# A decoder layer on one core: hidden tiles 4 and 5 computed as a pair, and another order of work in the opening

## The reference, cut to what matters

```
h = rms_norm(x, g_mix)
q, k, v, u, gate_a, gate_s = split(h @ w_in)       # 1024 -> 4096
attn_out = stick_breaking_attention(rms_norm(q), rms_norm(k), v) @ w_attn_out
y = gelu(s5(u));  ssm_out = (y @ w_glu_val) * sigmoid(y @ w_glu_gate)
x = x + (sigmoid(gate_a) * attn_out + sigmoid(gate_s) * ssm_out) @ w_out
x = x + square(relu(rms_norm(x, g_mlp) @ w_up)) @ w_down      # 1024 -> 4096 -> 1024
x = x + (p @ w_ple) * sigmoid(rms_norm(x, g_ple) @ w_ple_gate)
```

## Time and profile before

| what | value |
|---|---|
| median of 3 runs | 929.46 us (929.38 to 929.7) |
| the profiled execution | 929.17 us, span 927.5 us |
| PE busy | 912.6 us, 98% of the span, 7414 matmuls |
| DVE busy | 603.9 us, 65% |
| ACT busy | 442.1 us, 48% |
| POOL busy | 87.3 us, 9% |
| chain that ended last | PE 92%, DVE 3%, ACT 2%, issue 1% |

### The profile page before, as it was taken

The page is one execution under the profiler, slowest core; times in us unless marked ns, Lnnn a source line. Parts: engine busy times, 40 slices in busy tenths (PEclk is TensorE's granted clock), DMA queues, the critical chain, the costliest instruction groups (busy, mean ns, idle before and its releaser), DMA issues.

```text
span 927.5 us, 17663 instructions
## 1 busy us (share of the span) xinstructions
PE 912.6 (98%) x7414; PEld 886.1 (96%) x7414; DVE 603.9 (65%) x815; ACT 442.1 (48%) x663; POOL 87.3 (9%) x142
## 2 busy tenths in 40 slices
PE   6999999999999999999999999999999999999998
PEld 5999999999999889999999999999999999999998
DVE  6589699511777746475568666666676666778453
ACT  7546323223876544444356544444444444446532
POOL 5190032201001210100000000000000000000000
PEclk9999999999999999999999999999999999999999
DMA  9531554824523576522323222322323223242203
GB/s 234 126 87 44 149 166 105 192 74 154 131 71 96 197 277 213 170 70 69 92 69 92 90 84 83 89 90 91 91 75 92 87 90 92 91 137 71 69 5 99
DMA packets 134694, 102.19 MB, mean 110 GB/s; under 512 B 18560, under 2 KB 124408, under 8 KB 134584
## 3 DMA queue, kind: packets, MB, share of 16 engines
q1 hardware_dynamic: 129096, 83.38, 30.7%
q0 software_dynamic: 5424, 17.65, 6.0%
q10 hardware_dynamic: 96, 0.04, 0.0%
HBM read 88.71 MB, written 12.21 MB: 109 GB/s over the span
## 4 chain that ended last, share of the span: by engine, by line
PE 92%; DVE 3%; ACT 2%; issue 1%; DMA 0%; ACTq 0%; DVEq 0%
PE dense L2278 65%; PE banks L2278 20%; PE scoreA L2278 3%; PE banks L2434 2%; PE dense L2434 1%; PE scoreB L2278 1%; DVE Llo L1735 1%; ACT t L1616 1%; DVE t L2102 1%; ACT whi L1323 1%; DVE Ssum L1711 0%; DMA xtok<-in_x_sample 0%; DVE wlo L1735 0%; DVE sm L2160 0%; ACT yh L1662 0%
## 5 line engine op out<-in xcount | busy, mean ns | idle before, releaser
L1735 DVE TENSOR_TENSOR wlo<-wraw,whi 128x1024 fp32r<-128x1024 f32 (+1 forms) x139 | 152.6, 1102 | 104.2 <-ACT whi L1323 91.9
L2278 PE MATMUL dense<-hid,whi 128*128 128x256 f32 (+1 forms) x1024 | 176.6, 294 | 0.1
L2278 PE MATMUL dense<-act_hi,whi 128*128 128x256 f32 (+1 forms) x736 | 168.1, 298 | 1.4 <-issue 1.4
L2278 PE MATMUL dense<-act_hi,wlo 128*128 128x256 f32 (+1 forms) x736 | 164.6, 294 | 0.3 <-DVE wlo L1735 0.3
L2278 PE MATMUL dense<-act_lo,whi 128*128 128x256 f32 (+1 forms) x736 | 164.4, 294 | 0.0
L2278 PEld LDWEIGHTS dense<-hid,whi 128*128 128x128 f32 x1024 | 152.5, 188 | 0.5 <-issue 0.4
L1323 ACT CAST whi<-wraw 128x1024 fp32r<-128x1024 f32 x100 | 110.1, 1103 | 45.6 <-PE banks L2278 44.1
L2278 PEld LDWEIGHTS dense<-act_hi,whi 128*128 128x128 f32 x736 | 123.9, 188 | 4.8 <-issue 4.1
L2278 PEld LDWEIGHTS dense<-act_hi,wlo 128*128 128x128 f32 x736 | 124.6, 188 | 0.5 <-DVE wlo L1735 0.5
L2278 PEld LDWEIGHTS dense<-act_lo,whi 128*128 128x128 f32 x736 | 124.7, 188 | 0.0
L2278 PE MATMUL dense<-hid,wlo 128*128 128x256 f32 (+1 forms) x512 | 108.8, 294 | 0.0
(11 more groups left out here) (366 smaller groups left out, 1571.2 us busy)
## 6 DMA issues: line engine op xcount, KB each, us to landing
wraw<-in_w_in SPq DMA_DIRECT2D x32, 512.0 KB, 4.9
wraw<-in_w_up SPq DMA_DIRECT2D x32, 512.0 KB, 4.0
wraw<-in_w_down SPq DMA_DIRECT2D x32, 512.0 KB, 3.6
gates_spill<-gst POOLq DMA_DIRECT2D x16, 288.0 KB, 3.1
page<-in_cache_k SPq DMA_DIRECT2D x16, 256.0 KB, 7.9
page<-in_cache_v SPq DMA_DIRECT2D x16, 256.0 KB, 7.5
wraw<-in_w_out SPq DMA_DIRECT2D x8, 512.0 KB, 3.8
wraw<-in_w_ple_gate SPq DMA_DIRECT2D x8, 512.0 KB, 3.6
```

Source lines behind the costliest of these rows:

```text
L1735: return nc.vector.tensor_tensor(out=lo, in0=whole, in1=f32(hi), op=ALU.subtract)
L2278: return nc.tensor.matmul(out, lhsT, rhs, start=start, stop=stop, skip_group_check=True)
```

## The change: what it does

Two parts are changed together.

**Pair.** FIRSTPAIR becomes 4, so hidden tiles 4 and 5 are also one pair and there are 14 pairs. The units behind up 3 are now: D0, D1, pair 4, D2, pair 6, D3, pair 8, D4, D5, and so on: pairs 4 and 6 have one down unit behind each, the later ones two as before. In the event list, up 3 is followed by a flush (which holds the first two weight blocks of pair 4), by three of the four blocks of both halves of D0, and then by xpair 3, xsplit 2, rscale 2, xsplit 3, rscale 3, and only then by the rest of D0 half 0 and of half 1, rscale 6 and 7, and D1.

**Opening.** EVICT has an order for each half: 0, 2, 1, 3, 4, 6, 5, 7 for half 0, as before for half 1. ACT's copy of the first weights stands behind two tiles, not three. GpSimd subtracts 768 of the 1024 columns of the first `wlo`, DVE the other 256. GpSimd's tables come behind that. PE's first unit is reordered, and the second has an order of its own (all high x high, then high x low, then low x high).

```diff
-EVICT = (0, 2, 4, 6, 1, 3, 5, 7)
+EVICT = ((0, 2, 1, 3, 4, 6, 5, 7), (0, 2, 4, 6, 1, 3, 5, 7))
@@ units_of
     for f in range(8):
-        for i in range(0, 4, 2):
-            m, d = 4 * (f + 1) + i, [("down", 8 * f + 2 * n, 4, 2) for n in (i, i + 1)]
-            if m < FIRSTPAIR:
-                us += [("up", m, 8, 1), d[0], ("up", m + 1, 8, 1), d[1]]
-            else:
-                us += ([("pair", m, 8, 1), ("pair2", m + 1, 8, 1)] if f < 7 else []) + d
+        downs = [("down", 8 * f + 2 * n, 4, 2) for n in range(4)]
+        wide = [[("pair", m, 8, 1), ("pair2", m + 1, 8, 1)] if m < 32 else [] for m in (4 * f + 4, 4 * f + 6)]
+        if f == 0:
+            us += downs[0:2] + wide[0] + downs[2:3] + wide[1] + downs[3:4]
+        else:
+            us += wide[0] + downs[0:2] + wide[1] + downs[2:4]
-FIRSTPAIR = 6
+FIRSTPAIR = 4
@@ schedule_of
-    def pair():
+    def pair(downs):
...
-        for j in range(2):
+        for j in range(2 * downs):
             half_unit()
-            event("hidlow", m + j)
-        for j in range(2):
-            half_unit()
+            if j < 2:
+                event("hidlow", m + j)
...
         if half == 1:
+            event("pool_lo", 0)
             event("split_lo", 0)
-        for turn, k in enumerate(EVICT):
-            if half == 0 and turn == 3:
+        for turn, k in enumerate(EVICT[half]):
+            if half == 0 and turn == 2:
                 event("split_hi", 0)
...
     event("xsplit", 1)
     unit()
+    flush()
+    for j in range(2):
+        event("hpart", n[0], j, 0, 3)
     event("xpair", 3)
     event("xsplit", 2)
     event("rscale", 2)
-    unit()
     event("xsplit", 3)
     event("rscale", 3)
     half_unit(split_first=False)
-    flush()
-    half_unit()
+    half_unit(split_first=False)
     event("rscale", 6)
     event("rscale", 7)
-    unit(2)
+    unit()
     for m in range(FIRSTPAIR, 32, 2):
         if m == LASTHID - 8:
             event("inv")
-        pair()
+        pair(2 if m >= 8 else 1)
@@ gpsimd
+                if k == "pool_lo":
+                    pool.wait_ge(w_hi, turn["split", 0])
+                    tt(wlo[:, wslot(0), 0:LOW0], wraw[:, 0, 0:LOW0], f32(whi[:, wslot(0), 0:LOW0]),
+                       ALU.subtract).then_inc(count.up(pool_steps), 1)
+                    reached["w0_lo"] = count.last
+                    tables()
@@ vector
+                elif k == "split_lo":
+                    vector.wait_ge(w_hi, turn["split", 0])
+                    vector.wait_ge(*reached["w0_lo"])
+                    lower(wlo[:, wslot(0), LOW0:], wraw[:, 0, LOW0:],
+                          whi[:, wslot(0), LOW0:]).then_inc(count.up(w_lo), 1)
@@ tensor, first_unit
+                tensor.wait_ge(w_hi, turn["split", 0])
+                tensor.wait_ge(h_lo, EVICT[0].index(1) + 2)
+                high(0, 0, KT)
+                low_x(0, False)
+                high(1, 0, KT // 2)
+                tensor.wait_ge(w_lo, turn["split", 0])
+                low_w(0, 0, KT, True)
+                low_w(1, 0, KT // 2, False)
+                high(1, KT // 2, KT)
+                low_w(1, KT // 2, KT, False)
+                ins = low_x(1, True)
+            def second_unit():
+                tensor.wait_ge(w_hi, turn["split", 1])
+                slot = jobs["m", 1, 0][0] - DENSE
+                wh, wl = [wview(w, wslot(1), 1) for w in (whi, wlo)]
+                for turn_, (w, x) in enumerate(((wh, act[0]), (wh, act[1]), (wl, act[0]))):
+                    if turn_ == 2:
+                        tensor.wait_ge(w_lo, turn["split", 1])
+                    for k in range(KT):
+                        for c0, c1 in CUT:
+                            ins = mm(product_of(slot, c0, c1), w[:, k, 0:P], x[:, k, c0:c1],
+                                     start=turn_ == 0 and k == 0, stop=turn_ == 2 and k == KT - 1)
```

More of the change, by code:

```diff
@@ L1078, in _ @@
             sync.wait_ge(y_stored, 16 * 13)
+        LOW0 = 6 * P
         N_PARAMS = 14 + 2 * 4
@@ L1133, in _ @@
                                  ident[0:32, 0:32].unsqueeze(1).to_broadcast([32, 4, 32])).then_inc(count.up(pool_steps), 1)
[L1134 to L1157, removed]
             def load_x2(t):
@@ L1167, in load_p, with tables @@
                 pool.dma_start(ptok[0:n, t % 2, :], src).then_inc(x2_in[t % 2], 16)
+            def tables():
+                nc.gpsimd.memset(nrm[:], 1.0).then_inc(count.up(pool_steps), 1)
+                for half in range(2):
+                    nc.gpsimd.memset(f32(nrmr[half][:]), 0.0).then_inc(count.up(pool_steps), 1)
+                nc.gpsimd.memset(f32(selr[:]), 0.0).then_inc(count.up(pool_steps), 1)
+                sflat = sel[:, :, :].rearrange("r p c -> r (p c)")
+                nc.gpsimd.memset(sflat, 1.0).then_inc(count.up(pool_steps), 1)
+                pool.wait_ge(*count.last)
+                nc.gpsimd.affine_select(out=sflat, in_=sflat, compare_op=ALU.is_ge, fill=0.0, base=0,
+                                       pattern=[[1, 8 * P]], channel_multiplier=-64).then_inc(count.up(pool_steps), 1)
+                pool.wait_ge(*count.last)
+                nc.gpsimd.affine_select(out=sflat, in_=sflat, compare_op=ALU.is_ge, fill=0.0, base=63,
+                                       pattern=[[-1, 8 * P]], channel_multiplier=64).then_inc(count.up(pool_steps), 1)
+                pool.wait_ge(*count.last)
+                for r in (0, 32):
+                    nc.gpsimd.tensor_copy(selr[r:r + 16, :, :], sel[:, :, :]).then_inc(count.up(pool_steps), 1)
+                pool.wait_ge(*count.last)
+                nc.gpsimd.tensor_copy(stat[:, 2, 0:1], ident[:, 0:1]).then_inc(count.up(consts_ready), 1)
+                for row in range(SB):
+                    src = i["sb_bias"][0:1, 2 * (row // 2):2 * (row // 2) + 2].rearrange("a (h o) -> (a h) o", o=1)
+                    pool.dma_start(sbias[16 * row:16 * row + 16, :],
+                                   src.unsqueeze(1).to_broadcast([2, ST, 1])).then_inc(sbias_in, 16)
+                pool.dma_start(pti[:, :], i["page_table"].rearrange("b (n o) -> o (b n)", o=1)).then_inc(table_in, 16)
@@ L1169, in _ @@
             for e in schedule:
                 k, a = e[0], e[1:]
-                if k == "s5sq":
+                if k == "pool_lo":
[4 more added lines that the diff above has]
+                    tables()
+                elif k == "s5sq":
                     pool.wait_ge(s5_bb, 1)
@@ L1474, in _ @@
                     if m % 2:
-                        scalar.wait_ge(h_lo, KT * half + EVICT.index(m - 1) + 2)
+                        scalar.wait_ge(h_lo, KT * half + EVICT[half].index(m - 1) + 2)
                     nc.scalar.activation(act[0][:, m, c0:c0 + 2 * P], xview(half, m), ACT.Copy,
@@ L1883, in _ @@
                     c0 = 2 * P * half
-                    vector.wait_ge(h_hi, KT * half + EVICT.index(m) + 1)
+                    vector.wait_ge(h_hi, KT * half + EVICT[half].index(m) + 1)
                     nc.vector.scalar_tensor_tensor(out=act[1][:, m, c0:c0 + 2 * P], in0=xview(half, m),
@@ L1891, in _ @@
                             count.upto(*read(("xturned", half))), 1)
-                elif k in ("split", "split_lo"):
+                elif k == "split_lo":
[3 more added lines that the diff above has]
+                          whi[:, wslot(0), LOW0:]).then_inc(count.up(w_lo), 1)
+                elif k == "split":
                     split(a[0])
@@ L2303, in first_unit @@
                 wh, wl = [wview(w, 0, 0) for w in (whi, wlo)]
[L2305 to L2322, removed]
@@ L2323, in first_unit, with high, low_x @@
-                ins.then_inc(full_of(("m", 0, 0)), 1)
+                def high(half, n0, n1):
+                    c0, c1 = CUT[half]
+                    for n in range(n0, n1):
+                        k = EVICT[half][n]
+                        tensor.wait_ge(h_hi, KT * half + n + 1)
+                        mm(product_of(slot, c0, c1), wh[:, k, 0:P], act[0][:, k, c0:c1], start=n == 0)
+                def low_x(half, stop):
+                    c0, c1 = CUT[half]
+                    for n, k in enumerate(EVICT[half]):
+                        tensor.wait_ge(h_lo, KT * half + n + 2)
+                        ins = mm(product_of(slot, c0, c1), wh[:, k, 0:P], act[1][:, k, c0:c1],
+                                 stop=stop and n == KT - 1)
+                    return ins
@@ new lines, in low_w @@
+                def low_w(half, n0, n1, stop):
+                    c0, c1 = CUT[half]
+                    for n in range(n0, n1):
+                        k = EVICT[half][n]
+                        mm(product_of(slot, c0, c1), wl[:, k, 0:P], act[0][:, k, c0:c1], stop=stop and n == KT - 1)
+                tensor.wait_ge(w_hi, turn["split", 0])
[3 more added lines that the diff above has]
+                high(1, 0, KT // 2)
@@ new lines, in first_unit @@
+                tensor.wait_ge(w_lo, turn["split", 0])
[4 more added lines that the diff above has]
```

(8 more changed lines are left out.)

## The result

| kernel | median us | range, runs | profiled execution | mean granted clock |
|---|---|---|---|---|
| before | 929.42 | 929.02 to 929.7, 4 | 929.17 (span 927.5) | 1.00 |
| changed | 935.88 | 935.22 to 936.3, 4 | 935.22 (span 933.5) | 0.996 |

The ratio is 1.007 (95% interval 1.0058 to 1.0083): slower by 6.5 us. The prediction was 934.7.

The account below looks back on a forecast made before the run. PE, busy 98% of the span, was taken as the bound, so any new wait costs in full. -1.54 + 6.0 + 1.4 - 0.7 = +5.2 us gave a median of 934.7 us, range 931.0 to 937.0.

Parts of the forecast that it names:

- Matmuls removed, -1.54: Tiles 4 and 5 as one pair on PE: 11.10 us in place of 12.64, so -1.54 us.
- The wait, +6.0: Between D0 and D1 half 0, PE waits for DVE's late addition of D0 half 0 into R: 6.0 us.
- Behind the wait, nothing: From D1 and pair 4 on: no second wait, blocks lowered in time, weight loads cost nothing.
- PE's speed, +1.4: PE's matmuls behind the wait run slowly after the idle time: +1.4 us, bounds 0 and 2.5.
- The opening, -0.7: PE's first unit ends at 22.3 us, second unit earlier than 23.00: -0.7 us, bounds 0 and -1.4.
- GpSimd's share, no cost: Opening: GpSimd's 768-column subtraction takes 0.8 to 3.5 us, taken as under 3.0, so DVE is not held up.
- The late tables: GpSimd's tables start some 2.5 us later and end near 25; first PE user after 36 us, so no cost.
- The median: Whole kernel: 934.4 us for the profiled execution, plus 0.29 to the median of the runs, 934.7.
- the one at full pace: Rival: the wait before D1 comes, but PE restarts at once at full pace: 933.2 us; chance 0.28.
- the late GpSimd one: Rival: GpSimd's subtraction takes 5 us, DVE goes on 2 us later, opening +1.2: 936.6 us; chance 0.08.
- the one with a part of the wait hidden: Rival: DVE gets through work ahead earlier, hiding part of the wait: 929.5 to 932.5 us; chance 0.07.
- the rival of a short wait: Rival: wait before D1 short or absent, so faster, deciding at 2.2 us; 927.2 without any wait; chance 0.12.

Follow-up runs that it names:

- repaired kernel: Changed kernel with D0's two DVE additions ahead of xpair 3, PE's D0 reordered, rscale 6 and 7 behind pair 4, its blocks 4 to 6 behind its first product: 926.95 us.
- filler run: Changed kernel plus 40 extra matmuls of 288 rows into an unused PSUM bank between D0 and D1, result unread: 933.35 us.
- opening's order alone: Kernel before with the opening's new orders but without GpSimd's share, DVE subtracting all 1024 columns of the first low weights: 929.11 us.
- opening alone: Kernel before with the whole opening part, GpSimd's share included, and the pairs of before: 928.53 us.
- pair part alone: Kernel before with only the pair's edits and the opening of before: 936.12 us.
- kernel with 2.3 us: Changed kernel with both DVE additions of D0 ahead of xpair 3 and PE's D0 blocks reordered so half 0 ends earlier: 931.39 us.

## Why the prediction was right, step by step

The mechanism that makes the loss, the wait and the fallen clock behind it, is shown. That the size taken for the clock came near is in part luck.

- **Matmuls removed, -1.54.** The sum closes to 0.2 us with it. In the two profiles: -0.46 (lead at up 3's end, 492.57 against the earlier trace rows), +5.96 wait, +1.86 slow matmuls, -1.54 make +5.8; the difference of the profiled executions is 6.05. The repaired kernel, without wait, is 2.2 us under before, the -1.54 and -0.7 of the prediction.
- **The wait, +6.0.** 5.96 measured, in the place named, behind the addition named. DVE's list was also right line by line: shifted by the lead of 0.46, the forecast has xpair 3 done at 499.8, xsplit 3 and rscale 3 at 503.9, and the measured rows stand at 499.80 and 503.91. So no part of the wait was hidden. The experiments moved it to 3.9, 1.8 and 0 by moving what stands ahead of the addition.
- **Behind the wait, nothing.** Right for the changed kernel: no second wait shows. It was right only because of the wait itself: with the wait gone, 2.3 us turned up in pair 4, at ACT's psave copy. The prediction had said that pair 4's blocks have time; it did not name that copy.
- **PE's speed, +1.4.** The mechanism was right, the size too small: 1.86 at matmul starts, of which the filler run leaves 1.78 to the clock, and 2.2 to 2.5 between the medians. That 1.4 came so near is in part luck, since the 1.2 us it leaned on is not the price of slow transposes. The transposes were slow, as the durations of equal ones in the kernel before show (ns: least, median, most):

```profile
L2434 PE MATMUL dense<-ident,xtok x16: 417/418/473, 8.7 to 11.9; 128*128 128x128 f32 x16
L2434 PE MATMUL banks<-ident,xtok x16: 272/273/447, 12.2 to 14.2; 128*128 128x128 f32 x16
```

But both stretches that were compared are held by DVE's row tiles too. The first, 3.49 us, ends when the third row tile is scaled, at 12.12. In the run with the opening's order alone the first 16 were quicker, and PE then waited for that tile:

```profile
8.76 3.25 PE L2475 MATMUL dense<-ident,xtok 128*128 128x128 f32 x16 [0.47 <-DVE xtok L1871]
12.25 2.31 PE L2475 MATMUL banks<-ident,xtok 128*128 128x128 f32 x16 [0.24 <-DVE xtok L1871]
```

The second 16 start 7.57 us after the first square in both (12.18 - 4.61 and 12.25 - 4.68), so there the slow clock cost as good as nothing. The second stretch, 2.31 us, holds a pause for the fourth row tile (starts at 13.12 and then 13.40, where 0.11 is the step).
- **A slip in the same paragraph.** "PE is idle for 0.24 of 7.10 us busy" has the earlier trace rows the wrong way round: PE is busy for 0.24 of the 7.10 us. The comparison with a 6 us wait needs the idle time, so it stands.
- **The opening, -0.7.** 0.56 from the first row tile on and 0.64 in device time (929.17 to 928.53). DVE's 256 columns took 0.42 us as worked out. The lead of 0.46 at up 3's end is not all the opening's: 0.17 of it is there at the second unit, and the other 0.29 comes in a part of the list that the change leaves as it was. The opening alone leads by 0.38 and 0.32 at the same two places, so some 0.3 us is how executions differ.
- **GpSimd's share, no cost.** 1.83 us, between the bounds of 0.8 and 3.5, and DVE did not wait for it. The estimate from the figure of the Trainium skill, "GPSIMD Engine Reference", 3.1, was 1.7; the trace's 1.83 is near it. The late tables were costed at nothing too. They did lengthen a DVE subtraction (2.06 in place of 1.22 at 22.53), off the path.
- **The median.** 935.88 against 934.7. Of the 1.2 us, 0.5 is the slow matmuls (1.86 in place of 1.4), 0.2 the lead (0.46 in place of 0.7), 0.2 what the sum above doesn't place, and 0.4 the profiled execution, which lay 0.66 under the median where 0.29 had been put.

The rivals: the one at full pace, the late GpSimd one and the one with a part of the wait hidden are refuted above; the rival of a short wait is refuted for this list and realised by the repaired one.

## What to carry to other kernels

When the engine that bounds the kernel is busy without a gap, a new order costs whatever wait it makes, in full. A read that frees a buffer must be followed through the list of the engine that does it: count what stands ahead of it, not how busy that engine is. Removing one wait moves the question to the next engine's list, here from DVE's additions to ACT's copies, so walk all lists before a trial. A gap of 4 to 6 us on TensorE cost more than its length in every run here; where such a gap can't be avoided, try useless matmuls into a free bank, which here took off some 2 us. And when a price is read from two stretches of a trace, look first at what ends each of them: here another engine had a part in both.

## What the runs showed of the hardware

Whether the clock falls differs between runs of one kernel, and it fell in more runs where the wait was longer. By the longest wait of PE in the profiled execution, the mean clock was 0.998 or less in 2 of 10 runs with 1.8 us, in 8 of 11 with 2.3 us, in 5 of 5 with 3.9 us, in 8 of 8 with 6.0 us (the changed kernel and the pair part alone), and in 0 of 10 with none (repaired). In the kernel with 2.3 us the two groups lie 1.7 us apart in their middles (929.77 and 931.48), so a fall costs about as much there as the 1.78 us behind the 6 us wait.

GpSimd and DVE lengthen each other's passes when both read only SBUF, and mostly it is the one that starts second. DVE's 1024-column subtraction took 1.22 us with GpSimd idle, 1.78 when it started 0.34 us behind the table select, which kept its 1.03, and 2.06 when it started inside GpSimd's cast. GpSimd's two casts took 4.11 us together there, in place of 1.03 each. In the kernel before it was the other way round: DVE's subtraction started at 17.05 and kept its 1.22, and the second table select, started behind it, took 1.92:

```profile
16.14 1.03 POOL L1142 TENSOR_SCALAR_AFFINE_SELECT sel<-sel 16x1024 f32<-16x1024 f32 x1
17.24 1.92 POOL L1145 TENSOR_SCALAR_AFFINE_SELECT sel<-sel 16x1024 f32<-16x1024 f32 x1
```

DVE's tiles from PSUM were not lengthened by GpSimd's 768-column subtraction (four in 1.66 us, as without it).
